# Mixer C's projection steps in another order, and norm weights multiplied in as turned blocks leave PSUM

## The chip, the cores and the metric

The kernel runs on one core of a Trainium2 chip. The metric is the device time of one execution in microseconds (us), the median of several runs. TensorE multiplies and turns, VectorE and ScalarE do the elementwise work, GpSimd takes a small share of it, and SyncE issues all DMA. TensorE has two clock levels, 1.2 and 2.4 GHz; a granted clock of 0.50 in the rows is the lower one, 1.00 the higher.

## The reference

Two layers of a streaming encoder for 1024 prompt frames and 32 sample frames (1056 rows in nine tiles, the last of 32 rows). Each layer normalises x, projects it once for four mixers (A window attention, B differential attention, C latent attention, M cross-attention to 256 memory tokens), attends, projects the concatenated outputs, and ends with a convolutional feed-forward block. What matters here is C, and the queries of M:

```
def _rms(x, g):
    y = xf * lax.rsqrt(jnp.mean(xf * xf, axis=-1, keepdims=True) + EPS)
    return (y * g).astype(x.dtype)

cq = (_rms(cq, w["c_cq_g"]) @ w["c_wuq"]).reshape(B, S, C_HEADS, C_QK)          # rank 256 -> 4 heads x 96
cq = _rms(concatenate([cq[..., :64], _rope(cq[..., 64:], pos)]), w["c_qn_g"])
ckv = _rms(ckv, w["c_ckv_g"])                                                   # rank 128
cpe = _rope(cpe[:, :, None, :], pos)[:, :, 0]                                   # 32 wide, shared by the heads
kv = (ckv @ w["c_wukv"]).reshape(B, nk, C_HEADS, 64 + 64)
ck = _rms(concatenate([kv[..., :64], broadcast(cpe)]), w["c_kn_g"])
mq = _rms(mq.reshape(B, S, M_HEADS, HEAD_DIM), w["m_qn_g"])
```

The norm weight g multiplies after any rotation that stands inside the norm. For the queries and keys of C and the queries of M nothing but the weight comes between the normalised value and the attention, so it can be multiplied in before or after the block is turned.

## The kernel before

A layer runs through stages, each a block with one program per engine: M's projections, M's attention joined with B's projections, B's attention joined with A's projections, A's attention joined with C's projections, C's attention, the output projection (`w_o_block`), the feed-forward (`ffn_block`). Every matmul operand of the dense projections is split in a high and a low part, so each product takes three matmuls (L774 to L776).

`pieces_stage` builds a projection stage from pieces. A piece is one projection (its product, how its columns leave PSUM, its norm, how it is turned and where it goes), with a list of steps (first tile, tiles, rows). C has six pieces: `cq` (5 steps of two tiles, the last of 32 rows; dense, 48 matmuls of 256 columns for a full step), `q_up` (9 steps of one tile, from the turned `c_q_t`, 4 matmuls), `ckv` (5 steps, dense like `cq`, with a rotation of the 32 columns of cpe on VectorE), the prompt's keys (8 steps, 2 matmuls from the turned `ckv_t`), `lat` (4 steps that only turn cached latents) and the sample's keys (5 steps). Queries and keys of C are 4 heads of 96.

`order` is one list of (piece, step) which every engine follows; no planner moves anything. With g a place in this list, the engines' queues are:

- TensorE: product of step g+2, then the turns of step g (L808). A product from a turned tile waits until that tile's blocks have been copied (`placed`). The first two products stand inside the attention that comes before.
- ScalarE: `take(g+1)` copies the product out of PSUM (L855), waits for GpSimd's rotation if there is one, and squares (L866); `place(g-1)` writes the high part of the turned blocks (L894, or L903 for pieces with a plain copy); `root(g+1)` takes the square root (L876).
- VectorE: `results(g)` is a reciprocal (L1011), z by the reciprocal (L1015), by the norm weight (L1025), and for `ckv` the rotation of cpe (L970 to L974); `sum_squares(g+1)` (L992); `low_turned(g-1)`, the low part of the turned blocks (L1049).
- GpSimd: the rotation of the last 32 columns of each q head before the norm (L1079 to L1084).
- SyncE: weights and weights of norms, result writes, in the order of the list. The norm weights are loaded across all partitions, and scaled once (L952) if the piece has a scale.

z, the result and the root have two buffers each, taken in turn by the steps that have a norm. The weights of `ckv` are cast in the last `cq` step (L832, L944). For the keys ScalarE makes three copies: v, the 32 columns of cpe for four heads, and the 64 columns of k.

The order of C before is: the five `cq` steps; then q0, ckv0, q1, q2, ckv1, q3, q4, ckv2, q5, q6, ckv3, q7, q8, ckv4; then eight prompt keys, four `lat`, five sample keys.

## Time and profile before

| | |
|---|---|
| runs | 3252.74, 3257.39, 3262.34 us, median 3257.39 |
| the profiled execution | 3255.39 us, of which the span of the core 3253.6 us |
| TensorE busy | 2920.4 us (90%) |
| VectorE busy | 1807.6 us (56%) |
| ScalarE busy | 1197.6 us (37%) |
| GpSimd busy | 136.5 us (4%) |
| mean granted TensorE clock | 0.936 |
| C's projections after A's attention, first layer | 510 to 617 us |
| the same, second layer | 2111 to 2218 us |

The span is from the first to the last instruction; the execution's own time is 1.8 us more. All starts below are counted from the span's start. Busy times of different engines overlap. A matmul's row gives the modelled duration of one matmul, so rows of successive ones overlap, and the spacing of starts tells how fast they go. In square brackets stands how long the engine was idle before an instruction and what released it.

### The profile page before, as it was taken

How to read it: one execution, taken by the hardware profiler on the slowest of the kernel's cores; microseconds unless marked ns; L12 is line 12 of the kernel's file. 1: busy time of each engine (PE TensorE's matmuls, PEld its weight loads, DVE VectorE, ACT ScalarE, POOL GpSimd, SP SyncE). 2: the span in 40 equal slices, each digit the busy share in tenths (PEclk: the TensorE clock that was granted, in tenths of full speed). 3: DMA queues.
4: the chain of work that ended last, by engine and by line, in shares of the span. 5: the costliest groups of instructions: out<-in, count | busy, mean ns of one | idle time of the engine just before them, and what ended most of it. 6: DMA issues, size and time to landing. Idle time of an engine off the chain costs nothing. (4 is left out here: it accounts for less than half of the span.)

```text
span 3253.6 us, 49067 instructions
## 1 busy us (share of the span) xinstructions
PE 2920.4 (90%) x19080; PEld 2750.4 (85%) x19080; DVE 1807.6 (56%) x2899; ACT 1197.6 (37%) x2503; POOL 136.5 (4%) x228
## 2 busy tenths in 40 slices
PE   5888879789899999999968888788789999999997
PEld 3787768579899999999957868667789999999997
DVE  5466765643555555554665586465436555545554
ACT  5556644652322222222246474456413222212222
POOL 0200012000000000000002000120000000000000
PEclk7996989799999999999979979898899999999999
DMA  4110001022111111111031100110411111111111
GB/s 177 32 57 30 23 29 39 8 86 82 52 46 46 41 50 40 46 45 48 20 124 47 48 22 21 40 29 11 150 28 51 47 45 46 43 50 46 40 46 61
DMA packets 182436, 162.11 MB, mean 50 GB/s; under 512 B 14648, under 2 KB 170040, under 8 KB 181688
## 3 DMA queue, kind: packets, MB, share of 16 engines
q1 hardware_dynamic: 182200, 158.81, 15.5%
q8 instruction: 167, 2.74, 0.4%
q14 instruction: 69, 0.57, 0.1%
HBM read 129.92 MB, written 29.06 MB: 49 GB/s over the span
## 5 line engine op out<-in xcount | busy, mean ns | idle before, releaser
L1752 PE MATMUL ps<-h_hi,w_hi 128*128 128x352 f32 x2496 | 550.5, 329 | 49.6 <-DVE w_lo L1863 23.1
L1752 PE MATMUL ps<-h_hi,w_lo 128*128 128x352 f32 x2496 | 544.6, 325 | 6.9 <-issue 6.9
L1752 PE MATMUL ps<-h_lo,w_hi 128*128 128x352 f32 x2496 | 543.1, 326 | 0.0
L1752 PEld LDWEIGHTS ps<-h_hi,w_hi 128*128 128x128 f32 x2496 | 430.3, 192 | 64.7 <-issue 42.2
L1752 PEld LDWEIGHTS ps<-h_hi,w_lo 128*128 128x128 f32 x2496 | 433.3, 190 | 0.0
L1752 PEld LDWEIGHTS ps<-h_lo,w_hi 128*128 128x128 f32 x2496 | 429.7, 190 | 0.0
L2203 ACT ACTIVATE cv<-up,cols 128x1058 f32<-128x1058 f32 x88 | 112.0, 1273 | 737.9 <-issue 697.8
L774 PE MATMUL ps<-w_hi,h_hi 128*128 128x256 f32 (+1 forms) x1152 | 334.5, 290 | 24.1 <-DVE w_lo L944 18.2
L775 PE MATMUL ps<-w_lo,h_hi 128*128 128x256 f32 (+1 forms) x1152 | 328.8, 285 | 0.0
L776 PE MATMUL ps<-w_hi,h_lo 128*128 128x256 f32 (+1 forms) x1152 | 326.6, 284 | 0.0
L2314 DVE TENSOR_TENSOR x_t<-ps,x_t 128x1056 f32<-128x1056 f32 x176 | 221.0, 1256 | 159.5 <-PE ps L1752 158.8
L2280 DVE TENSOR_TENSOR up<-ps,rinv 128x704 f32<-128x704 f32 x88 | 78.4, 891 | 399.7 <-PE ps L1752 399.7
L1395 ACT ACTIVATE prob<-ps,nm 128x256 f32<-128x256 f32 (+8 forms) x360 | 224.2, 630 | 78.1 <-DVE nm L1309 54.4
L774 PEld LDWEIGHTS ps<-w_hi,h_hi 128*128 128x128 f32 (+1 forms) x1152 | 210.8, 183 | 30.2 <-issue 26.8
L1752 PE MATMUL ps<-act_hi,w_hi 128*128 128x352 f32 x1056 | 229.0, 325 | 5.1 <-issue 5.1
L1752 PE MATMUL ps<-act_lo,w_hi 128*128 128x352 f32 x1056 | 228.1, 324 | 0.0
L1752 PE MATMUL ps<-act_hi,w_lo 128*128 128x352 f32 x1056 | 228.1, 323 | 0.0
L2188 ACT CAST w_hi<-stage 128x1024 fp32r<-128x1024 f32 x132 | 136.0, 1043 | 247.8 <-PE ps L1752 240.8
L776 PEld LDWEIGHTS ps<-w_hi,h_lo 128*128 128x128 f32 (+1 forms) x1152 | 211.8, 184 | 0.9
L775 PEld LDWEIGHTS ps<-w_lo,h_hi 128*128 128x128 f32 (+1 forms) x1152 | 210.8, 183 | 0.8
L1309 DVE TENSOR_REDUCE nm<-ps 32x1 f32<-32x544 f32 (+10 forms) x234 | 184.0, 788 | 33.4 <-PE ps L1216 13.9
L1752 PEld LDWEIGHTS ps<-act_hi,w_hi 128*128 128x128 f32 x1056 | 180.2, 189 | 5.6 <-issue 5.6
(211 smaller groups left out, 4275.7 us busy)
## 6 DMA issues: line engine op xcount, KB each, us to landing
stage<-in_f_win SPq DMA_DIRECT2D x88, 512.0 KB, 3.8
stage<-in_f_wout SPq DMA_DIRECT2D x44, 512.0 KB, 3.7
stage<-in_w_in SPq DMA_DIRECT2D x40, 256.0 KB, 4.4
x_spill<-x_t SPq DMA_DIRECT2D x2, 4224.0 KB, 14.3
x_t<-x_spill SPq DMA_DIRECT2D x2, 4224.0 KB
stage<-in_w_o SPq DMA_DIRECT2D x16, 512.0 KB, 4.5
w_raw<-in_w_in SPq DMA_DIRECT2D x24, 256.0 KB, 3.9
o_in<-o_spill SPq DMA_DIRECT2D x8, 528.0 KB, 7.1
```

The costliest lines, as they stand in the source:

```text
L774: pe.matmul(out, h_hi[:, k, c:c + r], w_hi[:, k, :], start=(k == 0), stop=False)
L775: pe.matmul(out, h_hi[:, k, c:c + r], w_lo[:, k, :], start=False, stop=False)
L776: last = pe.matmul(out, h_lo[:, k, c:c + r], w_hi[:, k, :], start=False, stop=(k == KC - 1))
L1309: dve.tensor_reduce(nm[0:r, j % 4, 0:nh], v, AX.X, ALU.max, negate=True).then_inc(S.nm_done, 1)
L1395: last = act.activation(prob[0:r, j % 4, col:col + kn], src, ACT.Exp, bias=nm[0:r, j % 4, i:i + 1], accum_out=rsum[0:r, j % 4, i:i + 1])
L1752: last = pe.matmul(ps[:, s0 + b, 0:BAND], lh, rh_[:, b * BAND:(b + 1) * BAND], start=(first_k and n == 0), stop=(last_k and n == 2))
L2188: act.copy(w_hi[:, ws, :], stage[:, sg, :]).then_inc(S.hi_done, 1)
L2203: act.activation(cv[:, b, :], up[:, b, 2:UPC], ACT.Identity, scale=cols[:, 1, bass.ds(c, 1)], bias=cols[:, 1, bass.ds(c + 2 * FC, 1)]).the ...
L2280: dve.tensor_tensor(up[:, b, 2:2 + 2 * BAND].rearrange("p (t c) -> p t c", c=BAND), ps[:, s0:s0 + 2, 0:BAND], rinv[:, 0:2 * BAND].rearrang ...
L2314: dve.tensor_tensor(xm, ps[:, s0:s0 + 3, 0:BAND], xm, ALU.add).then_inc(S.x_added, 1)
```

## The change

Four things are changed.

1. A piece may have `late_gain`: C's q and both key pieces, and M's q. Its norm weight is loaded as one column with a value per partition. VectorE's `results` is then one multiplication by the reciprocal, straight into the result; ScalarE's `place` multiplies by the column as it copies, and VectorE's low part is one fused multiply and subtract.
2. C's keys get their 32 shared columns by a GpSimd copy (`shared`), in place of one of ScalarE's three copies. The square waits for it.
3. ScalarE copies k's columns first, then v's.
4. C's order is written out anew: cq0, cq1, cq2, q0, q1, cq3, q2, q3, cq4, q4, q5, ckv0, q6, q7, ckv1, q8, ckv2, k0, k1, lat0, ckv3, k2, k3, lat1, ckv4, k4, k5, lat2, k6, k7, lat3, then the five sample keys.

```diff
         def first_gains(sp):
             for p in normed:
-                sp.dma_start(p.gain_t[:, :], p.gain.partition_broadcast(P)).then_inc(S.small_loaded, 16)
+                if p.late_gain:
+                    for i in range(p.bw // p.hd):
+                        sp.dma_start(p.gain_t[i * p.hd:(i + 1) * p.hd, :], p.gain.rearrange("(h o) -> h o", o=1)
+                                     ).then_inc(S.small_loaded, 16)
+                else:
+                    sp.dma_start(p.gain_t[:, :], p.gain.partition_broadcast(P)).then_inc(S.small_loaded, 16)
...
-                    if p.rope_first:
+                    if p.rope_first or p.shared is not None:
                         act.wait_ge(S.pre_rotated, rot_i[g] + 1)
...
-                            act.copy(hi, src).then_inc(S.tr_copied, 1)
+                            if p.late_gain:
+                                if s == 0:
+                                    act.wait_ge(S.small_loaded, n_small)
+                                    if n_scaled[id(p)]:
+                                        act.wait_ge(S.gain_scaled, n_scaled[id(p)])
+                                act.mul(hi, src, p.gain_t[0:p.bw, 0:1]).then_inc(S.tr_copied, 1)
+                            else:
+                                act.copy(hi, src).then_inc(S.tr_copied, 1)
...
+                    if p.late_gain:
+                        dve.tensor_tensor(res[0:r, n % 2, 0:nt * n_el].rearrange("p (t h d) -> p t h d", t=nt, d=hd),
+                                          zv[:, :, 0:n_el].rearrange("p t (h d) -> p t h d", d=hd),
+                                          ri[0:r, 0:gh].rearrange("p (t h) -> p t h", t=nt).unsqueeze(3).broadcast_to([r, nt, H, hd]),
+                                          ALU.mult).then_inc(S.res_done, 1)
+                        return
...
-                    dve.tensor_tensor(lo, src, hi.bitcast(F32), ALU.subtract).then_inc(S.tr_low, 1)
+                    if p.late_gain:
+                        dve.scalar_tensor_tensor(lo, src, p.gain_t[0:p.bw, 0:1], hi.bitcast(F32), ALU.mult, ALU.subtract
+                                                 ).then_inc(S.tr_low, 1)
+                    else:
+                        dve.tensor_tensor(lo, src, hi.bitcast(F32), ALU.subtract).then_inc(S.tr_low, 1)
...
-                steps = [g for g in range(NG) if G[g][0].rope_first]
+                steps = [g for g in range(NG) if G[g][0].rope_first or G[g][0].shared is not None]
...
+                    if p.shared is not None:
+                        src, from_load, producer = p.shared(s)
+                        pool.wait_ge(S.res_done, n_i[g] - 1)
+                        if from_load:
+                            pool.wait_ge(S.data_loaded0, 16 * len(late_loads))
+                        else:
+                            q, qs = producer
+                            pool.wait_ge(S.res_done, n_i[at[id(q), qs]] + 1)
+                        zp = zs[0:r, n_i[g] % 2, 0:p.n_el].rearrange("p (h c) -> p h c", c=p.hd)
+                        pool.tensor_copy(zp[:, :, 64:96], src.unsqueeze(1).broadcast_to([r, 4, 32])).then_inc(S.pre_rotated, 1)
+                        continue
...
-                return [(v_big[0:r, v_tile(t0), :].rearrange("p (h c) -> p h c", c=64), b4[:, :, 64:128]),
-                        (z4[:, :, 64:96], cpe_of(t0, r).unsqueeze(1).broadcast_to([r, 4, 32])),
-                        (z4[:, :, 0:64], b4[:, :, 0:64])]
+                return [(z4[:, :, 0:64], b4[:, :, 0:64]),
+                        (v_big[0:r, v_tile(t0), :].rearrange("p (h c) -> p h c", c=64), b4[:, :, 64:128])]
...
-        order = [(cq, s) for s in range(5)]
-        for s in range(5):
-            order += [(q_up, 2 * s), (ckv, s)] + ([(q_up, 2 * s + 1)] if s < 4 else [])
-        order += [(p, s) for p in pieces[3:] for s in range(len(p.steps))]
+        k_p, k_c = pieces[3], pieces[5]
+        order = [(cq, 0), (cq, 1), (cq, 2), (q_up, 0), (q_up, 1), (cq, 3), (q_up, 2), (q_up, 3), (cq, 4), (q_up, 4), (q_up, 5),
+                 (ckv, 0), (q_up, 6), (q_up, 7), (ckv, 1), (q_up, 8), (ckv, 2), (k_p, 0), (k_p, 1), (lat, 0), (ckv, 3),
+                 (k_p, 2), (k_p, 3), (lat, 1), (ckv, 4), (k_p, 4), (k_p, 5), (lat, 2), (k_p, 6), (k_p, 7), (lat, 3)]
+        order += [(k_c, s) for s in range(5)]
```

## Rows read from the trace of the kernel before

**Rows 1.** Stretches of C's projections: length, busy (count) per engine, PEclk, DMA share, GB/s.

```profile
538.00:549.00 11.00, 10.09 (x70) 8.42 (x70) 6.91 (x19) 4.75 (x14) 4.65 (x11) 1.00 0.07 17
578.00:598.50 20.50, 14.10 (x47) 6.33 (x47) 19.09 (x50) 16.25 (x50) 0.00 (x0) 0.83 0.01 2
```

**Rows 2.** Timeline of the stage's end: start, duration, engine, line, instruction, count.

```profile
614.29 0.30 ACT L876 ACTIVATE rt<-ss,eps_c 32x4 f32<-32x4 f32 x1 [0.29 <-DVE ss L992]
...
617.02 0.29 DVE L1049 TENSOR_TENSOR kc_s<-ps,kc_s 96x128 fp32r<-96x128 f32 x1 [0.31 <-ACT kc_s L894]
```

**Rows 3.** TensorE's timeline over one period of ckv and two q steps.

```profile
537.83 0.44 PE L808 MATMUL ps<-ident,res 128*128 128x128 f32 x2 [0.86 <-DVE cpe_all L974]
...
543.84 0.60 PE L808 MATMUL ps<-ident,res 128*96 128x128 f32 x4
...
548.49 0.44 PE L808 MATMUL ps<-ident,res 128*128 128x128 f32 x2 [0.91 <-DVE cpe_all L974]
```

**Rows 4.** ScalarE's timeline over the same period, the roots.

```profile
539.46 0.30 ACT L876 ACTIVATE rt<-ss,eps_c 128x4 f32<-128x4 f32 x1
...
543.81 0.30 ACT L876 ACTIVATE rt<-ss,eps_c 128x4 f32<-128x4 f32 x1 [0.30 <-DVE ss L992]
...
545.96 0.30 ACT L876 ACTIVATE rt<-ss,eps_c 128x2 f32<-128x2 f32 x1 [0.57 <-DVE ss L992]
```

**Rows 5.** Timeline of one key step on ScalarE and VectorE.

```profile
582.80 0.30 ACT L876 ACTIVATE rt<-ss,eps_c 128x4 f32<-128x4 f32 x1 [0.63 <-DVE ss L992]
...
583.44 0.56 DVE L1015 TENSOR_TENSOR u<-zs,ri 128x384 f32<-128x384 f32 x1
...
584.03 0.56 DVE L1025 TENSOR_TENSOR res<-u,gain 128x384 f32<-128x384 f32 x1
...
584.97 0.68 DVE L1049 TENSOR_TENSOR k_st<-ps,k_st 96x512 fp32r<-96x512 f32 x1
...
585.77 0.56 DVE L1015 TENSOR_TENSOR u<-zs,ri 128x384 f32<-128x384 f32 x1
```

**Rows 6.** Lines of the output projection: duration in ns min/median/max, first and last start.

```profile
L1831 ACT ACTIVATE h_hi<-ps,subln_c x12: 287/682/691, 745.2 to 2348.9; 128x512 fp32r<-128x512 f32 x8, 128x32 fp32r<-128x32 f32 x4
L1833 ACT CAST h_hi<-ps x12: 186/587/595, 735.7 to 2339.3; 128x512 fp32r<-128x512 f32 x8, 128x32 fp32r<-128x32 f32 x4
L1875 DVE SCALAR_TENSOR_TENSOR h_lo<-ps,subln_c,h_hi x12: 250/742/751, 746.4 to 2349.3; 128x512 fp32r<-128x512 f32 x8, 128x32 fp32r<-128x32 f32 x4
```

**Rows 7.** Timeline of the first sample key step on ScalarE and VectorE.

```profile
603.59 0.52 ACT L866 ACTIVATE sq<-zs 128x384 f32<-128x384 f32 x1
...
604.14 0.55 DVE L992 TENSOR_REDUCE ss<-sq 128x4 f32<-128x384 f32 x1 [3.10 <-ACT sq L866]
604.73 0.30 ACT L876 ACTIVATE rt<-ss,eps_c 128x4 f32<-128x4 f32 x1 [0.47 <-DVE ss L992]
...
605.79 0.52 ACT L866 ACTIVATE sq<-zs 128x384 f32<-128x384 f32 x1
```

**Rows 8.** ScalarE's timeline at the end of the cq steps.

```profile
517.24 0.63 ACT L903 COPY c_q_t<-ps 128x256 f32<-128x256 f32 x2
518.09 0.30 ACT L876 ACTIVATE rt<-ss,eps_c 128x2 f32<-128x2 f32 x1 [0.22 <-DVE ss L992]
...
525.69 2.17 ACT L832 CAST w_hi<-stage 128x512 fp32r<-128x512 f32 x4
```

**Rows 9.** VectorE's timeline at the end of M's projections.

```profile
110.25 0.41 DVE L1025 TENSOR_TENSOR res<-u,gain 32x256 f32<-32x256 f32 x1
```

**Rows 10.** Stretches around a change of the granted clock, columns as in rows 1.

```profile
574.40:577.80 3.40, 0.81 (x2) 0.00 (x0) 1.73 (x5) 2.07 (x7) 0.44 (x1) 1.00 0.00 0
577.80:584.50 6.70, 6.58 (x15) 2.86 (x15) 5.70 (x20) 4.97 (x18) 0.00 (x0) 0.50 0.02 3
```

**Rows 11.** C's attention in the first and the second layer, columns as in rows 1.

```profile
618.40:711.00 92.60, 92.05 (x660) 85.09 (x660) 43.54 (x140) 51.27 (x129) 0.00 (x0) 0.89 0.04 13
2219.00:2311.00 92.00, 87.29 (x660) 80.90 (x660) 43.60 (x141) 51.26 (x129) 0.00 (x0) 0.93 0.05 14
```

More of the change, by code:

```diff
@@ L161, in build_program @@
         loads_done = sem("loads_done")
+        gain_scaled = sem("gain_scaled")
         fin_done = sem("fin_done")
@@ L495, in piece @@
                  rope_first=False, rope_extra=False, gain=None, scale=None, cached=None, raw=None, stack=None, to=None,
-                 res_out=None, v_out=None, placed=None)
+                 res_out=None, v_out=None, placed=None, late_gain=False, shared=None)
         p.update(args)
@@ L514, in __init__ @@
             self.gain_t, self.scale = None, p["scale"]
+            self.late_gain, self.shared = p["late_gain"], p["shared"]
         @property
@@ L581, in pieces_stage @@
         for p in normed:
-            p.gain_t = (gains or w).take("gain", [P, p.hd])
+            p.gain_t = (gains or w).take("gain", [P, 1 if p.late_gain else p.hd])
         G = order or [(p, s) for p in pieces for s in range(len(p.steps))]
@@ L606, in pieces_stage @@
         a_i = count(lambda p: p.after)
-        rot_i = count(lambda p: p.rope_first)
+        rot_i = count(lambda p: p.rope_first or p.shared is not None)
         normed_steps = [g for g in range(NG) if G[g][0].normed]
@@ L623, in pieces_stage @@
                     split_after[last_of[id(holders[i - 1])]] = p
-        n_small = 16 * len(normed)
+        n_small = 16 * sum(p.bw // p.hd if p.late_gain else 1 for p in normed)
         n_loads = 16 * len(loads)
+        n_scaled, scaled = {}, 0
+        for p in normed:
+            scaled += 1 if p.scale is not None else 0
+            n_scaled[id(p)] = scaled
         res_sem = (S.res_out0, S.res_out1)
@@ L1078, in gpsimd @@
                         pool.wait_ge(S.pre_rotated, i)
+                    turned_steps += 1
                     pool.tensor_tensor(a[:, :, 0:16], x1, cos, ALU.mult)
@@ L1581, in group_m @@
             piece(PAIRS, w_col=COL["mq"], copies=zs_copy, zsw=256, H=4, hd=HD, gain=I["m_qn_g"][layer], scale=HD ** -0.5,
-                  stack="after", to=lambda t: (q2_hi, q2_lo, t * P)),
+                  late_gain=True, stack="after", to=lambda t: (q2_hi, q2_lo, t * P)),
             piece([(0, 1, P), (1, 1, P)], H=4, hd=HD, cached=lambda s: kc[:, s, :],
@@ L1706, in pieces_c, with keys @@
         lat = piece([(t, 1, P) for t in range(4)], raw=lambda s: lat_in[:, s, :], stack="raw", to=lambda t: (ckv_s, None, t * P))
-        def keys(steps, latents, cpe_of, v_tile, placed, to):
+        def keys(steps, latents, shared, v_tile, placed, to):
             def product(pe, t, r, out):
@@ L1714, in copies @@
                 z4 = zs.rearrange("p t (h c) -> p (t h) c", c=96)
-                return [(v_big[0:r, v_tile(t0), :].rearrange("p (h c) -> p h c", c=64), b4[:, :, 64:128]),
-                        (z4[:, :, 64:96], cpe_of(t0, r).unsqueeze(1).broadcast_to([r, 4, 32])),
-                        (z4[:, :, 0:64], b4[:, :, 0:64])]
+                return [(z4[:, :, 0:64], b4[:, :, 0:64]),
+                        (v_big[0:r, v_tile(t0), :].rearrange("p (h c) -> p h c", c=64), b4[:, :, 64:128])]
             return piece(steps, product=product, placed=placed, zw=512, zsw=384, copies=copies, H=4, hd=96,
-                         gain=I["c_kn_g"][layer], stack="after96", to=to)
+                         gain=I["c_kn_g"][layer], stack="after96", to=to, late_gain=True, shared=shared)
         pieces = [
             cq, q_up, ckv,
-            keys(SINGLES[:-1], lambda t, r: ckv_t[:, t * P:t * P + r], lambda t, r: cpe_all[0:r, t, :], lambda t: t,
+            keys(SINGLES[:-1], lambda t, r: ckv_t[:, t * P:t * P + r], lambda s: (cpe_all[:, s, :], False, (ckv, s // 2)), lambda t: t,
                  lambda s: (ckv, s // 2), lambda t: (k_st[:, 0::2, :], k_st[:, 1::2, :], t * P)),
@@ L1728, in pieces_c @@
                  lambda t, r: ckv_s[:, t * P:t * P + r] if t < 4 else ckv_t[:, SEQ:T],
-                 lambda t, r: cpe_s[0:r, t, :] if t < 4 else cpe_all[0:r, PT_TILES, :], lambda t: PT_TILES + t,
+                 lambda s: (cpe_s[:, s, :], True, None) if s < 4 else (cpe_all[0:DEC, PT_TILES, :], False, (ckv, 4)),
+                 lambda t: PT_TILES + t,
                  lambda s: (lat, s) if s < 4 else (ckv, 4), lambda t: (k_s[:, 0::2, :], k_s[:, 1::2, :], t * P)),
         ]
-        order = [(cq, s) for s in range(5)]
-        for s in range(5):
-            order += [(q_up, 2 * s), (ckv, s)] + ([(q_up, 2 * s + 1)] if s < 4 else [])
-        order += [(p, s) for p in pieces[3:] for s in range(len(p.steps))]
+        k_p, k_c = pieces[3], pieces[5]
[3 more added lines that the diff above has]
+        order += [(k_c, s) for s in range(5)]
         return pieces_stage(layer, pieces, R_W2, order=order, joint=FOUR_HEADS,
```

9 lines of the change are left out of this document (7 added, 2 removed).

## Prediction

> **What bounds the kernel now.** I read the table of busy times first: TensorE works 90% of the span, VectorE 56%, ScalarE 37%. That is an average over stages, so I cut the stage of mixer C into stretches [rows 1]. Up to 571 us TensorE is busy 10.09 of 11 us; later it is not: from 578 to 598.5 it is busy 14.10 of 20.5, part of that at the low clock of 1.2 GHz (granted 0.83 in the mean), and VectorE is the full one, 19.09 of 20.5. So the stage has a dense part, set by TensorE or near it, and a light part of some 45 us after the last ckv product, set by the chain of the norm: ScalarE copies z out of PSUM, squares it, VectorE sums, ScalarE takes the root, VectorE scales, TensorE turns, ScalarE and VectorE write high and low part. The stage's last write ends at 617.31 [rows 2]. The second layer has the same stage, 108 us long too.
>
> Then the timeline of one period with two q steps and one ckv step [rows 3]: turns of ckv stand at 537.83 and 548.49, 10.66 us apart, and TensorE is idle 0.86 and 0.91 us before them, for VectorE's last rotary add. The dense product takes 538.02 to 543.84, 5.82 us. The reader is to see that even the dense part hangs on the chain, by a little. ScalarE's roots give the chain's pitch [rows 4]: 539.46 to 543.81 is 4.35 us for a second q step, 543.81 to 545.96 is 2.15 for ckv, and what is left of the 10.66 is 4.16 for the other q step. (A q step is long because ScalarE waits in it until GpSimd has rotated.)
>
> A key step lasts 2.33 us [rows 5], from 583.44 to 585.77 on VectorE, which has no idle time between.
>
> **Late weights (the gain).** 22 steps of a layer in C (9 q, 13 keys) and 5 in M lose VectorE's multiplication by the gain: 0.59 us from 583.44 to 584.03 is what it adds before the result is there [rows 5], 0.35 for 32 rows of M. Instead the place on ScalarE takes a per-partition factor, and the low part becomes a fused multiply and subtract. The trace has both forms in the output projection [rows 6]: 682 against 587 ns on ScalarE, 742 ns on VectorE against the 0.68 of the plain subtract in [rows 5]. So +0.10 and +0.06 us a step. ScalarE's extra lies beside the sum and root of the same step (the square starts 1.14 before the root [rows 7], square and place take 0.43 + 0.67 of it), so it costs nothing there; if the cover fails, 22 x 0.1 = 2.2 us a layer.
>
> **GpSimd copies the shared key part.** One of three copies leaves ScalarE's key step, 0.20 us of the 1.06 from a root to the next square [rows 7]. The new GpSimd copy of 128 x 128 is not in the trace: nothing if hidden, 0.5 us if exposed (ScalarE's own copy of it is the nearest: its 0.20 is the spacing, so 0.5 is a bound with a wait's latency in it). It may start when the result of two steps before is there, a whole step early, so I take nothing.
>
> **New pitch of a key step.** In [rows 7], where the sum did not queue behind VectorE's other work: square 603.59, root 604.73 (1.14), next square 605.79 (1.06 with three copies, 0.86 with two). So 2.00 us, ScalarE and VectorE in turn; VectorE's own work is 2.33 - 0.59 + 0.06 = 1.80, so it no longer sets it. A ckv step after q steps falls from 2.15 to 1.65, since the q result it queues behind comes 0.59 earlier and the longer place takes back 0.1.
>
> **The new order.** TensorE's queue is: product of step g+2, then turn of g. I follow the roots from 518.09, which both kernels share [rows 8].
> - q0 now stands right after cq2. Its product needs cq0's blocks in c_q_t, written at 517.24 + 0.63 = 517.87 [rows 8]. Product 1.4, so the copy is at 519.45, and its root at 519.45 + 3.95 = 523.4. New stall, TensorE idle 1.6.
> - q1 4.35, cq3 2.2, q2 4.16, q3 4.35: 538.4. cq4 carries the cast of the ckv weights, 2.17 on ScalarE [rows 8] and as long again on VectorE behind it: 4.1, so 542.5. q4, q5 8.5: 551.0. ckv0 1.65, q6, q7 8.5, ckv1 1.65, q8 4.4: 567.3.
> - ckv1's product could start 2.72 after ckv0's root, 555.4, and ends at 561.2; then come a turn, q8's product and q7's turn, 2.2 (two turns and two products take 3.74 in [rows 3], 4.65 less the idle 0.91). ckv2's product runs 563.4 to 569.25, so here TensorE is the later one by 2.0.
> - Now the critical place. From the end E of a dense ckv product: copy, square, sum and root start 0.2, 0.46, 0.45 and 0.44 after one another (from the spacings of these rows and the half width of ckv's), so root at E + 1.55; the turn comes 2.53 after the root (545.96 to 548.49, [rows 3, 4]). VectorE is free for the sum of the first key step only then (E + 3.92), its root follows 0.59 later [rows 7], at E + 4.5, and its turn after 1.25 (582.80 to 583.44, 0.56 of work, 0.05 to the turn [rows 5]), and after 0.45 of turning, E + 6.2, TensorE may start the product of ckv3: the lat step beside it has no product, so ckv3 stands in TensorE's queue behind the turn of that key step. The period is 5.82 + 6.2 = 12.0, not the some 9 us that the products and turns would fill. So ckv3 runs 575.5 to 581.3, ckv4 (32 rows, half as long) 587.6 to 590.6.
> - Root of the fifth key step: 590.6 + 3.8 = 594.4, by the same steps with the 32-row results of ckv4, an estimate. Eight key steps remain at 2.0, and the product after a lat step is late twice by about 0.8, as it waits for the turn of the key step three before: 594.4 + 16 + 1.6 = 612.0. From the last root, 614.29, to the end took 3.0 in the old kernel [rows 2], now 0.59 less: 614.4.
>
> The old order had one more cost that goes: the four lat turns stood in one row, with VectorE idle 3.10 us before the sum of 604.14 [rows 7].
>
> Sum in C: 617.3 to 614.4, -2.9 us a layer. Much of what the interleaving hides (ckv3 and ckv4 beside key steps) comes back as waits of 5.7 and 2.8 us of those steps for the dense products.
>
> In M the projection's tail ends on the chain: the gain at 110.25, 0.41 us before the last results, is gone [rows 9], and the mul costs 0.1: -0.35. One more small load in M's queue, about 0.5 us of SyncE, lies ahead of w_mem, whose first use is later than its landing by the copies of mem_t; if that cover is gone, +0.5. C's gain loads are as many as before (five), and 4-byte rows; no step needs them for 50 us. The late loads of C now start at ckv0, 542 us, and the first key product is at 570: hidden.
>
> Work of both layers: 2 x (-2.9 - 0.35) = -6.5 us.
>
> **The clock.** TensorE was busy 0.81 of 3.40 us, then the granted clock fell to 0.50 and stayed there for 6.7 us [rows 10]. Today that falls on a light part that VectorE sets, and costs little. In the new order each lull after a dense ckv product (little to do in its last 3.7 us but two turns) is followed by a dense product, which at 1.2 GHz takes twice as long: 6.7 us of it cost 3.4. The light part from 578 to 598.5, idle a third of its time, was granted 0.83: such a lull is sometimes followed by the fall and sometimes not [rows 1]. There are two such lulls before ckv3 and ckv4 and a smaller one before ckv0. I take one fall a layer that costs 2 us after what other waits absorb: +4. Bounds: 0, and three a layer, 2 x (3.4 + 3.4 + 3) = +19.6.
>
> The Trainium skill, "TensorE: Matmul & The Clock Gate", section "HAM oscillation — how this bites in real kernels", says that bursts of matmuls parted by waits can run at the low clock each time anew, and it advises to keep dense work together. That speaks against this order. By it every lull would be paid, which is the upper bound, +19.6; by the rows, of which the periods with gaps of 0.9 us ran at 1.00 throughout [rows 1], only some.
>
> The profiled execution took 3255.39 us, 1.8 above its span and 2.0 below the median 3257.39. Its sum: 3255.4 - 6.5 + 4 = 3252.9; on the median's footing 3254.9. I say 3254.
>
> **Rivals.**
> 1. *The worked chain, one fall a layer (the forecast)*: 3254, own range 3248 to 3259. Chance 0.50.
> 2. *No fall under a dense product*: 3257.4 - 6.5 = 3251. For it: the q periods kept 1.00 with their gaps. Chance 0.20.
> 3. *The lull is filled*: the first key step's sum gets ahead of ckv's rotation, or the product of ckv3 is issued before that turn. Then each period is about 9 instead of 12, twice a layer, and the key steps wait less: -12 more, 3239. Against it: both queues are in written order. Also here: C's attention starts at half clock for longer in the first layer than in the second, TensorE 92.05 against 87.29 us busy for the same 660 matmuls [rows 11]; if the first gets the short one, -4.8 more. Together 0.18 for 3236 to 3247.
> 4. *Slower: the clock falls in every lull before a dense product.* Place: ckv0, ckv3 and ckv4 of both layers; price 19.6 in all, 3257.4 - 6.5 + 19.6 = 3270.5. It decides once the falls cost over 6.5 + 9.8 = 16.3 us, so nearly all have to come. For it: the fall at 577.8 came after just such a lull. Against it: products of q and keys still stand in most of the lull. Chance 0.12. The rule of the Trainium skill quoted above gives this outcome.
>
> **Numbers.** A measurement of this kernel can tell about 0.3%, 9.8 us, from no change: 3247.6 and 3267.2. Faster: nearly all of rival 3 and a bit of 2, 0.21. Slower: 0.09 of rival 4 and an unforeseen wait, 0.10. Same: 0.69. Range: from within rival 3 to short of rival 4's end, 3240 to 3266.
>
> **What would show it.** The stage from 510 us to the end of key writes in C should last about 105 us instead of 107.3; the gain's multiplication should be gone from q and key steps; key roots 2.0 apart at the end; TensorE idle about 1.6 us before the first q product; 6.2 us from the end of ckv2's product to the start of ckv3's; lat turns without a wait of their own; whether the clock is 0.50 within ckv3. I am wrong if the lull before ckv3 is much shorter, if q periods are no longer 10.2 to 10.7 us, or if the place with a factor lands on the chain.

## The result and the profile after

The kernel after takes 3293.42 us (3273.57 to 3310.11, 13 runs) against 3257.68 of the kernel before (3249.49 to 3285.07, 13 runs): a ratio of 1.0096, 95% interval 1.0071 to 1.0121. It is slower, and above the forecast's range. The profiled execution took 3294.7 us, 39.3 more than that of before; the mean granted clock fell from 0.936 to 0.926.

TensorE's busy time rose by 32 us (2920.4 before), for the same 19080 matmuls:

```profile
PE 2952.1 (90%) x19080; PEld 2785.4 (85%) x19080; DVE 1784.9 (54%) x2845; ACT 1196.7 (36%) x2477; POOL 141.1 (4%) x254
```

C's attention in both layers, the stretches of [rows 11] (length, busy per engine, granted clock, DMA share, GB/s):

```profile
621.86:736.05 114.19, 114.18 (x660) 105.43 (x660) 43.23 (x139) 51.02 (x129) 0.00 (x0) 0.70 0.03 10
2243.05:2349.28 106.23, 106.22 (x660) 97.98 (x660) 43.23 (x139) 51.10 (x129) 0.00 (x0) 0.76 0.03 11
```

From its first to its last matmul it lasts 114.19 and 106.23 us where it lasted 92.06 and 87.29: +41.1 us, more than the whole loss. The change does not touch this stage. Cut at the changes of the clock (the return stands at 689.73), first layer, kernel after:

```profile
618.04:621.86 3.82, 0.58 (x5) 0.42 (x5) 2.29 (x5) 1.18 (x4) 0.00 (x0) 0.50 0.00 0
621.86:689.90 68.04, 68.04 (x280) 63.74 (x281) 24.74 (x90) 27.00 (x74) 0.00 (x0) 0.50 0.03 8
689.90:736.05 46.15, 46.14 (x382) 41.69 (x381) 18.48 (x49) 24.02 (x56) 0.00 (x0) 1.00 0.04 12
```

and of the kernel before:

```profile
615.37:618.43 3.06, 0.53 (x4) 0.42 (x5) 1.59 (x4) 0.30 (x2) 0.00 (x0) 0.50 0.00 0
618.43:639.20 20.77, 20.77 (x86) 19.59 (x86) 10.75 (x47) 10.18 (x34) 0.00 (x0) 0.50 0.04 13
639.20:710.49 71.29, 71.29 (x577) 65.47 (x575) 32.52 (x93) 41.05 (x95) 0.00 (x0) 1.00 0.04 12
```

In both the clock falls in the light tail, 3 to 4 us before the attention. Then TensorE is busy without a gap, yet stays at 0.50 for 20.8 us in one kernel and 68.0 in the other. The Trainium skill ("TensorE: Matmul & The Clock Gate", Part 1) has the granted clock follow how busy TensorE has lately been. A row of 68.04 us busy in 68.04 at 0.50 does not agree, if busy is read as the profile shows it.

The projections themselves, kernel after. TensorE waits before q0's product, and between ckv2's product (it ends at 572.86, where a turn follows) and the first matmul of ckv3's (578.86):

```profile
520.66 1.53 PE L1740 MATMUL ps<-w_uq,c_q_t 128*128 128x384 f32 x4 [1.52 <-ACT c_q_t L921]
...
576.78 0.44 PE L819 MATMUL ps<-ident,res 128*128 128x128 f32 x2 [1.32 <-DVE cpe_all L994]
578.47 0.64 PE L819 MATMUL ps<-ident,res 128*96 128x128 f32 x4 [1.25 <-DVE res L1036]
578.86 0.36 PE L785 MATMUL ps<-w_hi,h_hi 128*128 128x256 f32 x1
```

Key steps and the stage's end, on ScalarE, VectorE and GpSimd, answering to [rows 2] and [rows 5]: the gain's multiplication is gone, the low part takes 0.74 us, the GpSimd copy 0.29.

```profile
577.22 0.30 ACT L887 ACTIVATE rt<-ss,eps_c 128x4 f32<-128x4 f32 x1 [1.16 <-DVE ss L1012]
577.86 0.56 DVE L1036 TENSOR_TENSOR res<-zs,ri 128x384 f32<-128x384 f32 x1
579.22 0.30 ACT L887 ACTIVATE rt<-ss,eps_c 128x4 f32<-128x4 f32 x1 [0.30 <-DVE ss L1012]
580.34 0.74 DVE L1077 SCALAR_TENSOR_TENSOR k_st<-ps,gain,k_st 96x512 fp32r<-96x512 f32 x1
580.48 0.29 POOL L1111 COPY zs<-cpe_all 128x128 f32<-128x128 f32 x1 [3.41 <-DVE res L1036]
...
617.96 0.30 ACT L887 ACTIVATE rt<-ss,eps_c 32x4 f32<-32x4 f32 x1
620.37 0.34 DVE L1077 SCALAR_TENSOR_TENSOR kc_s<-ps,gain,kc_s 96x128 fp32r<-96x128 f32 x1 [0.35 <-ACT kc_s L910]
```

The clock at 0.50 inside the projections of the first layer, where ckv0's product takes 7.1 us in place of 5.8 and ckv4's 4.2 in place of some 3:

```profile
543.10:549.90 6.80, 5.43 (x20) 3.92 (x19) 4.76 (x12) 3.80 (x9) 2.20 (x6) 0.51 0.35 87
590.90:594.30 3.40, 3.40 (x18) 2.84 (x17) 1.83 (x4) 1.14 (x3) 0.29 (x1) 0.52 0.00 0
```

### The profile page after: what moved, and what is told of

It is laid out like the page before. It is cut to its first block and busy times, and to the rows that moved or that the text cites. A ratio compares the mean times of both kernels' runs of the same rounds, so it can differ in the third digit from the quotient of the medians.

```text
span 3292.9 us, 49051 instructions
## 1 busy us (share of the span) xinstructions
PE 2952.1 (90%) x19080; PEld 2785.4 (85%) x19080; DVE 1784.9 (54%) x2845; ACT 1196.7 (36%) x2477; POOL 141.1 (4%) x254
## 5 line engine op out<-in xcount | busy, mean ns | idle before, releaser
L1456 ACT COPY pt<-ps 128x512 f32<-128x512 f32 (+5 forms) x306 | 127.7, 457 | 181.3 <-PE ps L1279 181.3
```

The source lines that it names most:

```text
L1456: act.copy(pt[0:kn, p % 2, grp[0]:grp[0] + len(grp), 0:r], ps[0:kn, 4 + g % 2, 0:len(grp) * P].rearrange("p (m c) -> p m c", c=P)[:, :, 0: ...
```

## The experiments

Eighteen more kernels were measured. Four measures are read from each profile, beside the time. "Proj" is the work of C's projections, from the root of cq2 to the last root (518.09 to 614.29 before: 96.2 us). "Att" is C's attention from first to last matmul, first/second layer. "Start" is where that first matmul stands against the last fall of the clock before it or the first one inside the attention: +3.1 is 3.1 us behind it, -2.0 means that the clock fell 2.0 us into the attention. "Low" is the time at 0.50 inside the attention. The moments of fall and return are read to a few hundredths of a us, from stretches that end or begin there. Times taken at different hours differ by some us; each ratio is against runs of before taken beside it.

| kernel | us (range, runs) | ratio to before, 95% | Proj | Att | Start | Low |
|---|---|---|---|---|---|---|
| before, profiled run | 3255.39 | | 96.2/96.2 | 92.1/87.3 | +3.1/+3.0 | 21/11 |
| after, profiled run | 3294.70 | | 97.2/97.2 | 114.2/106.2 | +3.8/+3.7 | 68/51 |
| e1 old order, late weights | 3234.39 (3226.83-3249.02, 10) | 0.9924 [0.9892, 0.9955] | 89.4/89.4 | 87.4/87.3 | +2.8/+2.9 | 11/11 |
| e2 new order alone | 3263.18 (3259.19-3291.45, 10) | 1.0025 [0.9987, 1.0063] | 102.6/102.7 | 90.8/87.4 | +2.4/+2.8 | 18/11 |
| e3 after, filled | 3237.55 (3231.74-3277.61, 10) | 0.9964 [0.9928, 0.9999] | 99.9/99.9 | 83.2/83.2 | no fall | 0/0 |
| e4 before, filled | 3254.25 (3229.68-3269.26, 10) | 0.9969 [0.9929, 1.0009] | 96.2/96.4 | 86.1/115.0 | -2.9/-3.1 | 7/68 |
| f1 before, 0.6 us wait | 3281.36 (3260.45-3305.42, 8) | 1.0079 [1.0050, 1.0109] | 96.2/96.2 | 114.3/91.8 | +3.7/+3.5 | 68/20 |
| f2 after, 1.1 us wait | 3265.97 (3254.21-3275.72, 10) | 1.0025 [1.0008, 1.0042] | 100.0/97.3 | 96.2/96.0 | +4.5/+5.0 | 30/29 |
| f3 after, 2.2 us wait | 3262.90 (3254.84-3267.49, 10) | 1.0020 [1.0010, 1.0030] | 97.3/97.4 | 87.4/92.1 | +6.2/+6.5 | 11/21 |
| f4 e1, filled | 3223.10 (3220.42-3231.80, 4) | 0.9910 [0.9892, 0.9929] | 88.4/88.4 | 91.9/87.3 | +3.3/+3.0 | 21/11 |
| g1 e1, lat turns between keys | 3236.64 (3232.53-3268.77, 10) | 0.9931 [0.9894, 0.9967] | 89.0/89.1 | 90.8/116.6 | +2.3/+2.2 | 18/73 |
| g2 e1 without GpSimd's copy | 3249.21 (3243.55-3261.09, 10) | 0.9973 [0.9939, 1.0006] | 92.2/92.3 | 90.9/95.8 | +2.3/+1.9 | 18/29 |
| g3 f4, B filled too | 3222.97 (3219.71-3229.01, 4) | 0.9886 [0.9810, 0.9961] | 90.6/88.4 | 83.2/92.0 | none/+3.3 | 0/21 |
| g4 new order up to ckv2 | 3267.33 (3241.64-3288.72, 10) | 1.0015 [0.9972, 1.0057] | 92.9/94.4 | 114.2/104.4 | +3.7/+4.2 | 68/47 |
| h1 e1, 0.6 us wait | 3246.95 (3240.20-3275.20, 11) | 0.9973 [0.9947, 0.9998] | 89.4/89.4 | 106.2/106.3 | +3.7/+3.6 | 51/51 |
| h2 after, filled at the end only | 3266.88 (3255.06-3297.20, 10) | 1.0038 [1.0007, 1.0070] | 97.4/100.0 | 95.5/103.6 | -1.6/-1.8 | 27/44 |
| h3 e1, filled more | 3214.42 (3207.69-3223.20, 4) | 0.9865 [0.9819, 0.9912] | 88.8/88.8 | 83.2/83.2 | no fall | 0/0 |
| h4 g1, filled more | 3219.05 (3216.22-3221.31, 4) | 0.9875 [0.9834, 0.9917] | 89.0/89.1 | 83.2/83.2 | no fall | 0/0 |
| i1 before, filled more | 3274.58 (3259.07-3285.74, 12) | 1.0060 [1.0037, 1.0083] | 95.3/96.8 | 108.4/105.2 | -2.0/-2.1 | 55/48 |
| i2 after, filled more | 3238.39 (3235.70-3260.35, 11) | 0.9960 [0.9940, 0.9981] | 96.3/96.2 | 89.3/86.1 | -3.0/-2.9 | 14/7 |

### Undo the order, or make it alone (e1, e2)

e1 is the kernel after with the old list:

```diff
-        k_p, k_c = pieces[3], pieces[5]
-        order = [(cq, 0), (cq, 1), (cq, 2), (q_up, 0), ...
+        order = [(cq, s) for s in range(5)]
+        for s in range(5):
+            order += [(q_up, 2 * s), (ckv, s)] + ([(q_up, 2 * s + 1)] if s < 4 else [])
+        order += [(p, s) for p in pieces[3:] for s in range(len(p.steps))]
```

> The kernel after with C's order put back to the old one; the late norm weights, the smaller projection pieces of ScalarE and GpSimd's copy of the shared columns stay. Where the two profiles differ by 39 us, some 42 us lie in C's attention, whose instructions are the same in both: it stays at the granted clock 0.50 for 71.7 and 54.6 us from the fall before it, against 23.9 and 13.7 us. Theory A, the new order brings this (the steps before the attention come at another rhythm): here it is gone, and what is left is the shorter steps, 3250 to 3258 us. Theory B, the short key steps at the stage's end bring it (turns 2.0 us apart in place of 2.33): it stays, 3280 to 3300. Theory C, neither edit but the moment at which the attention starts: the time scatters by 20 us and more from run to run, anywhere from 3250 to 3300, and the span goes with the mean granted clock.

e2 is the kernel before with the new list.

> The kernel before with the new order alone: norm weights and ScalarE's three copies of a key step as before, key steps 2.33 us. Theory A (the order): C's attention stays at 0.50 for over 50 us, 3285 to 3305 us. Theory B (the short key steps): attention as before, and the stage itself about as long as in the kernel before or some 2 us longer, 3255 to 3265. Theory C (the moment of the start): scatter of 20 us and more from run to run.

e1 came out 20 us below the kernel before, beyond what theory A gave. e2's median, 3263.18 us, lies in theory B's range, but not for B's reason: its projections are 6.4 us a layer longer where B had at most 2, and two of its ten runs, 3285 and 3291, lie where A had put all of them. Proj gives the work: late weights and the smaller key step take 6.8 us a layer off in the old order (96.2 to 89.4) and 5.4 in the new one (102.6 to 97.2); the new order costs 6.4 with early weights and 7.8 with late ones. Nothing of this is 41 us. A and B both fell: the new order alone has a short stay at 0.50 (18 and 11 us, against A), and so have the short key steps in the old order (11 and 11, against B).

The roots around the turns of the cached latents in e1 (ScalarE), and its attention:

```profile
589.06 0.30 ACT L887 ACTIVATE rt<-ss,eps_c 128x4 f32<-128x4 f32 x1
591.06 0.30 ACT L887 ACTIVATE rt<-ss,eps_c 128x4 f32<-128x4 f32 x1
598.10 0.30 ACT L887 ACTIVATE rt<-ss,eps_c 128x4 f32<-128x4 f32 x1 [0.47 <-DVE ss L1012]
```

```profile
609.98:697.34 87.36, 87.35 (x660) 80.93 (x660) 43.28 (x139) 51.20 (x129) 0.00 (x0) 0.94 0.04 13
2200.62:2287.96 87.34, 87.34 (x660) 80.92 (x660) 43.28 (x139) 51.19 (x129) 0.00 (x0) 0.94 0.04 13
```

A key step is 2.00 us here, as worked out.

### Fill the tail (e3, e4)

```diff
+                    if len(late_loads) == 3 and g >= NG - 9:
+                        warm(pe, 2)          # pe.matmul(ps[:, 0, 0:512], h_hi[:, 0, 0:P], h_hi[:, 0, 0:512]), unread
                     turn(g)
+                if len(late_loads) == 3:
+                    warm(pe, 6)
```

> The kernel after with extra matmuls at the end of C's projections, whose results nobody reads: two of 128 x 512 before each of the last nine turns, six behind the last one, where TensorE otherwise waits. Theory D, the attention is slow because the clock has already fallen in the light tail ahead of it: with the tail filled the clock is 1.00 when the attention starts, and stays there; both attentions lose all their time at 0.50, (71.7 + 54.6) x 0.47 = 59 us, some 3235 to 3240 us. Against it: the attention itself is what cannot hold the clock; then it falls anyway soon after the start, and the time is 3285 to 3310.

> The kernel before with the same extra matmuls. Theory D: (23.9 + 13.7) x 0.47 = 18 us less, 3238 to 3242 us, which would put it level with the same filling in the kernel after, less the 6 us of work that the change takes out. Otherwise 3255 to 3300 with the clock at 0.50 in the attention as often as before.

e3 took 56 us less than the kernel after (3293.42, at another hour), with no work removed. Its attention never falls:

```profile
621.62:704.79 83.17, 82.93 (x660) 76.17 (x660) 43.28 (x139) 50.95 (x129) 0.00 (x0) 1.00 0.04 14
```

So 83.2 us is this attention at full clock, and each us at 0.50 adds 0.39 to 0.46 ((87.3 - 83.2) / 10.6, (114.2 - 83.2) / 68.0). In e4 the filling carried the clock over the start, but it fell 2.9 and 3.1 us later and stayed down for 68.3 us in the second layer. Its ten times lie from 3230 to 3269, their median 3254.25 above the 3238 to 3242 expected. Filling acts on the cause, but does not hold the clock in every run.

### Move nothing but the start (f1, f2, f3, h1)

```diff
                 low_turned(NG - 1)
+                if len(late_loads) == 3:
+                    for _ in range(1):       # f1, h1: 1, f2: 2, f3: 4
+                        link(dve.tensor_tensor(u[:, 0:384], sq[:, 0:384], sq[:, 0:384], ALU.mult))
```

The extra multiplications stand behind everything else that VectorE does for C's projections, so they put off the attention and nothing ahead of it.

> The kernel before with one extra VectorE multiplication of 128 x 384 (some 0.56 us), read by nobody, behind the last low part of C's projections: C's attention starts that much later, nothing else moves. In the profiles so far the attention starts 3.13 and 3.0 us behind the moment at which the granted clock fell in the kernel before, and goes back to 1.00 after 20.8 and 10.7 us; in the kernel with the old order and late weights 2.98 and 3.02 us behind it, back after 10.7 and 10.7; with the new order alone 2.25 and 2.56, back after 18.2 and 11.1; in the kernel after 3.66 and 3.45, back after 68 and 51 us. Theory E, what decides is where the start lies against the moment of the fall: here it lies 3.6 us behind it, the attention stays at 0.50 for over 40 us a layer, and the time goes up by 20 to 45 us, to 3275 to 3300. Rival F, it is what the tail of the stage does (shorter steps, other distances of turns): nothing but the added time, 3254.1 + 1.1 = 3255.

> The kernel after with two such multiplications (1.1 us) behind the last low part. Theory E: the start moves from 3.55 to 4.7 us behind the fall; the attention should find the clock back sooner, and the time falls by 20 to 40 us to 3252 to 3275, though 1.1 us a layer are added. Rival F: 3293 + 2 = 3295.

> The same with four (2.2 us). Theory E: again a shorter stay at 0.50, 3253 to 3275; two waits of different length both helping would say that only a narrow place of the start is bad. Rival F: 3293 + 4 = 3297.

> Old order, late weights and GpSimd's copy (3234 us; its attention starts 3.0 us behind the fall and is back at 1.00 after 10.7 us in both layers), with one VectorE multiplication of some 0.56 us behind the last low part. Theory E (the place of the start decides, and 3.4 to 3.7 us behind the fall is a bad one in the kernels before and after): 51 to 68 us at 0.50, 20 to 27 us more a layer, 3260 to 3290 us. Rival: this stage's tail is robust, and the gain of 20 us is its own: 3235 to 3240.

f1, the kernel before with 0.54 us of idle work on VectorE, has in its first layer the kernel after's attention, all but instruction for instruction (280 and 281 matmuls in the low stretch); in the second it stays low for 20 us:

```profile
617.73 0.54 DVE L1062 TENSOR_TENSOR u<-sq 128x384 f32<-128x384 f32 x1
```

```profile
615.89:619.63 3.74, 0.53 (x5) 0.42 (x5) 2.04 (x5) 0.30 (x2) 0.00 (x0) 0.50 0.00 0
619.63:687.80 68.17, 68.17 (x281) 63.87 (x281) 24.77 (x90) 27.17 (x75) 0.00 (x0) 0.50 0.03 8
```

It lost 26 us in the median for 1.1 us of added work. And the kernel after gets faster by waiting: 27 us with 1.1 us a layer, 31 with 2.2, against the 3293.42 of an earlier hour (f3's attention, both layers):

```profile
624.15:711.54 87.39, 87.39 (x660) 80.97 (x660) 43.29 (x139) 51.25 (x129) 0.00 (x0) 0.94 0.04 13
2225.28:2317.36 92.08, 92.07 (x660) 85.09 (x660) 43.29 (x139) 51.24 (x129) 0.00 (x0) 0.89 0.04 12
```

Rival F, that the content of the tail decides, is out: in these kernels it is the same. Theory E holds in direction. The distances in its text (3.66, 2.98 and so on) came from coarser stretches; read at the fall itself they are those of the table. Second layers of f1 and h1, and the first of the kernel after:

```profile
2240.43:2240.63 0.20, 0.00 (x0) 0.00 (x0) 0.17 (x2) 0.00 (x0) 0.00 (x0) 1.00 0.00 0
2240.63:2244.15 3.52, 0.52 (x4) 0.42 (x5) 1.83 (x4) 0.30 (x2) 0.00 (x0) 0.50 0.00 0
2218.64:2218.84 0.20, 0.00 (x0) 0.00 (x0) 0.17 (x2) 0.12 (x1) 0.00 (x0) 1.00 0.00 0
2218.84:2222.47 3.63, 0.53 (x4) 0.42 (x5) 1.93 (x4) 0.40 (x2) 0.00 (x0) 0.50 0.00 0
617.84:618.04 0.20, 0.20 (x3) 0.00 (x0) 0.17 (x2) 0.16 (x2) 0.00 (x0) 1.00 0.17 41
```

Of the forty attentions in the twenty profiles, 25 start while the clock is down from a fall ahead of them. In order of the distance, with kernels described further down:

| start behind the fall, us | low, us | attentions |
|---|---|---|
| 1.91 | 29 | g2 second |
| 2.20 | 73 | g1 second |
| 2.34 to 2.40 | 18 | g1, g2 and e2 first |
| 2.75 to 3.00 | 11 | e2 second, e1 both, f4 second, before second |
| 3.06 to 3.52 | 20 to 21 | before first, g3 second, f4 first, f1 second |
| 3.63 to 3.68 | 51 | h1 both, after second |
| 3.70 to 3.82 | 68 | g4 first, f1 first, after first |
| 4.19 | 47 | g4 second |
| 4.52, 4.97 | 30, 29 | f2 |
| 6.17, 6.45 | 11, 21 | f3 |

Different kernels share a row. So in these profiles the distance tells how long the clock stays down, and between 3.52 and 3.63 us the stay jumps from 20 to 51. This orders 25 starts; it does not say why.

The times of theory E are less sure: h1 lost 12.6 us against e1, not 26 to 56; its profiled run, 3275.20 with 51 us low in both layers, is the slowest of eleven, and eight of the others show a mean clock of 0.939 or 0.940, close to e1's. Where their attentions started against the fall is not known, as only the profiled run has a trace.

### What each part of the work is worth (g1, g2, g4)

g2 puts ScalarE's three copies back into e1, g4 changes the new list behind ckv2, and g1 takes the old list to ckv4 and then spreads the cached latents:

```diff
 # g2
-                return [(z4[:, :, 0:64], b4[:, :, 0:64]),
-                        (v_big[0:r, v_tile(t0), :]..., b4[:, :, 64:128])]
+                return [(v_big[0:r, v_tile(t0), :]..., b4[:, :, 64:128]),
+                        (z4[:, :, 64:96], cpe_of(t0, r).unsqueeze(1).broadcast_to([r, 4, 32])),
+                        (z4[:, :, 0:64], b4[:, :, 0:64])]
 # g4
-                 (ckv, 0), (q_up, 6), (q_up, 7), (ckv, 1), (q_up, 8), (ckv, 2), (k_p, 0), (k_p, 1), (lat, 0), (ckv, 3), ...
+                 (ckv, 0), (q_up, 6), (q_up, 7), (ckv, 1), (q_up, 8), (ckv, 2), (ckv, 3), (ckv, 4)]
+        order += [(p, s) for p in pieces[3:] for s in range(len(p.steps))]
 # g1
+        for s in range(4):
+            order += [(k_p, 2 * s), (k_p, 2 * s + 1), (lat, s)]
```

> Old order, late norm weights, but ScalarE makes its three copies of a key step in the old order and GpSimd none. My working gave a key step 1.06 + 1.14 = 2.20 us where ScalarE and VectorE take turns, against 2.00 with two copies and 2.33 before. Then 13 x 0.2 = 2.6 us a layer of the gain are the GpSimd copy's, and the stage lasts 2.6 us longer than with both. If GpSimd's copy is worth nothing because VectorE or the wait for it sets the step, the roots stand 2.00 apart here too.

> The kernel after with the new order of cq, q and ckv up to ckv2, then ckv3, ckv4, and keys and cached latents as in the old order. From the root of cq2 to the last root of C's projections the kernel after takes 97.2 us, the old order with late weights 89.4. Theory G, the cost of 7.8 us lies between ckv2 and the last key (waits before ckv3 and ckv4, a dense product behind a key's turn): here 90 to 92. Theory H, it lies in the early q steps (1.5 us stall before q0, q steps while the next cq weights are cast): here 95 to 97.

> The kernel after with the old order up to ckv4, then the turns of cached latents one behind each two prompt keys as in the new order, then the sample's keys. In the old order with late weights the roots on both sides of the four turns stand at 591.06 and 598.10, 7.04 us apart where 2.00 is a key step; in the new order one such turn costs 0.8 us (607.15 to 609.98). So the stage should last 5.0 - 4 x 0.8 = 1.8 us a layer less than with the old order, 105.6 where the old order has 107.4 or so. The total depends besides on where the attention's start falls against the clock: if about 3.0 us behind the fall as in the old order, 3231; if the fall stays and the start moves to 1 or 4.5 us behind it, anything from 3230 to 3265.

g2's key roots stand 2.20 apart, as expected:

```profile
578.61 0.30 ACT L887 ACTIVATE rt<-ss,eps_c 128x4 f32<-128x4 f32 x1 [0.79 <-DVE ss L1012]
580.82 0.30 ACT L887 ACTIVATE rt<-ss,eps_c 128x4 f32<-128x4 f32 x1 [0.55 <-DVE ss L1012]
583.02 0.30 ACT L887 ACTIVATE rt<-ss,eps_c 128x4 f32<-128x4 f32 x1
```

So of the 6.8 us a layer, 4.0 are the late weights' (96.2 to 92.2) and 2.8 those of GpSimd's copy with the smaller ScalarE step. (g2 also puts back the old sequence of ScalarE's copies, v first, so the two are not told apart.) g4 stands between G and H: 3.5 us lie in the early part (first layer; the second, with a fall of the clock in it, 5.0), the other 4.3 between ckv2 and the last key, the clock's price on ckv4 among them. g1 gained 0.4 us, not 1.8: the key steps behind the four lat turns take 3.9, 2.6, 2.9 and 2.8 us and one more 2.5 in place of 2.0 each, 4.7 in all, nearly the 5.0 that four turns in a row cost.

### Filling again, and a version faster than both (f4, g3, h2, h3, h4, i1, i2)

f4 is e1 with e3's filling; g3 adds six matmuls behind B's projections; h2 is the kernel after with `warm(pe, 14)` at the end and none between turns; h3 (on e1), h4 (on g1), i1 (on before) and i2 (on after) fill more:

```diff
-                    if len(late_loads) == 3 and g >= NG - 9:
-                        warm(pe, 2)
+                    if len(late_loads) == 3 and g >= NG - 13:    # h2: warm(pe, 0)
+                        warm(pe, 3)
                     turn(g)
-                if len(late_loads) == 3:
-                    warm(pe, 6)
+                if len(late_loads) == 3:                         # g3: or over_results is not None, warm(pe, 6)
+                    warm(pe, 8)                                  # h2: 14
```

> Old order, late norm weights and GpSimd's copy (3234 us by itself), with the extra matmuls at the stage's end. The first of these had C's attention at 0.50 for 10.7 us a layer. If the filling holds the clock as it did in the kernel after (3293 to 3238), 2 x 10.7 x 0.47 = 10 us less: 3224 to 3228. If it fails in some runs as in the kernel before (3230 to 3236 or 3261 to 3269), two groups of times, 3225 and 3255, and a median anywhere between.

> Old order, late weights, GpSimd's copy and the extra matmuls in C (3223 us), with six more of 128 x 512 behind the last turn of B's projections. B's attention starts at 0.50 in all profiles, 44.4 and 37.5 us of it in the kernel before, on a stretch where VectorE is as full as TensorE. If the extra matmuls keep the clock up, some 5 to 20 us less, 3205 to 3218; if B's attention cannot hold it, no change.

> The kernel after with fourteen matmuls of 128 x 512 behind the last turn, none between the turns. If the tail between the turns is where the clock falls, it falls all the same 3 to 4 us before the attention, the fourteen run at 0.50 (0.43 us each, some 6 us, about 3 us more than the wait that is there today), and the attention starts later and at another place: 3250 to 3300, the profile tells. If it is the gap behind the last turn alone that brings the fall, no fall: 3293 - 2 x 27 = 3240.

> Old order with late weights; three matmuls of 128 x 512 before each of the last thirteen turns and eight behind the last one (two, nine and six in the kernel of 3223 us, whose profile still showed falls 3.3 and 3.0 us before the attention). If that holds the clock: C's attention 83.2 us in both layers, where the profile of 3223 us had 91.9 and 87.3: 13 us less, 3210. The filling may cost up to 0.2 us a key step where TensorE had too little room, 5 us in all: 3215. If the clock falls anyway, 3223 to 3250.

> The same filling with the turns of the cached latents between the prompt keys (3237 us without filling; from the root of cq2 to the last root 89.0 us against 89.4). Held clock: 3210 to 3214, within 1 us of the one before. Without it, anything up to 3260.

> The kernel before with three extra matmuls of 128 x 512 before each of the last thirteen turns of C's projections and eight behind the last. If C's attention is held at 1.00 in both layers: 83.2 us each in place of 92.1 and 87.3, 13 us less, 3242 us, or some 14 more than the old order with late weights and the same filling, since its stage is 6.8 us a layer longer: 3214 + 14 = 3228. The two ways disagree by 14 us; which is right says how much of 3214 comes from elsewhere. If the fall comes just behind the attention's start, as in the first filling of this kernel: up to 3265.

> The kernel after with the same filling. Held clock: 3237 as with the lighter filling, or up to 5 us more where the filling takes room that dense products want. Against the kernel before with the same filling: from the root of cq2 to the last root it took 99.9 us with the lighter filling against 96.2, so it should be 2 x 3.7 = 7 us slower; without any filling the two stood at 97.2 and 96.2, 2 us. That is the change without the clock: no gain, a loss of 2 to 7 us.

f4's attention started behind falls as e1's did, so its 11 us below e1 are not explained by C's attention; the two were also measured at different hours. Filling B changed nothing that can be told (3223.1 and 3223.0). h2 shows the tail between the turns to be where the clock goes: with the end filled alone it fell all the same, 8.7 and 8.4 us before the attention, came back, and fell again inside it. h3 is the fastest of all, 1.35% below the kernel before (0.9865, 0.9819 to 0.9912, four runs), with the clock at 1.00 in both attentions:

```profile
608.13:691.33 83.20, 82.95 (x660) 76.20 (x660) 43.28 (x139) 50.94 (x129) 0.00 (x0) 1.00 0.04 14
2191.72:2274.89 83.17, 82.93 (x660) 76.18 (x660) 43.27 (x139) 50.93 (x129) 0.00 (x0) 1.00 0.04 14
```

h4 has both attentions at 83.2 us too, but took 3219.05 us, above the 3210 to 3214 expected; its ratio of 0.9875 (0.9834 to 0.9917) can't be told from h3's.

The same filling in the kernel before is no remedy: i1 was meant to show the work with the clock taken out, and failed at that. In its first layer, the filled gap, the attention's first 2 us, and what follows:

```profile
618.50:623.10 4.60, 3.50 (x8) 2.42 (x9) 0.39 (x2) 0.30 (x2) 0.00 (x0) 0.66 0.00 0
623.10:625.10 2.00, 1.75 (x13) 1.62 (x14) 1.28 (x7) 1.99 (x6) 0.00 (x0) 0.99 0.04 8
625.10:679.70 54.60, 54.60 (x224) 50.89 (x224) 20.66 (x75) 21.25 (x62) 0.00 (x0) 0.50 0.03 10
```

and i2's attentions:

```profile
617.24:706.55 89.31, 89.06 (x660) 82.02 (x660) 43.28 (x139) 50.91 (x129) 0.00 (x0) 0.92 0.04 13
2211.40:2297.54 86.14, 85.89 (x660) 79.19 (x660) 43.28 (x139) 50.91 (x129) 0.00 (x0) 0.96 0.04 14
```

With one filling in both, the kernel after (i2) is 36 us faster than the kernel before (i1); without it, 36 us slower. The sign of the comparison is the clock's. By its work the change is about nothing: taking from each profiled execution what its attentions exceed 2 x 83.2 us leaves 3242 for before and 3241 for after. The same sum gives 3235 for i1 and 3228 for i2, and 3226 for e4 and 3232 for e3, so it is sure to some 7 us only, either way.

## Why the prediction was wrong

**The step that failed** is "The clock". It priced a fall only where one of C's dense products runs under it (+4 us, 19.6 at most), and its fourth rival summed those falls alone. What fell and stayed low was the stage behind, C's attention: +41.1 us in the profiled run. The row that could have warned was on the table: 92.05 and 87.29 us for the same 660 matmuls [rows 11]. I used it as a possible gain of 4.8 us in rival 3 and set no loss against it. Had I asked how long that stay could get, the bound would have been the whole attention at 1.2 GHz; from the rows of before alone, 92.05 us at a mean of 0.89, nothing excluded it. This one term is nearly the whole miss: in the terms of the profiled runs the forecast was 3252.9, and 3294.70 is 41.8 above it.

**The outcome** had the sign of rival 4 but not its mechanism. The rule of the Trainium skill quoted there ("TensorE: Matmul & The Clock Gate", section "HAM oscillation — how this bites in real kernels"), lulls before dense work, came true only in part: the clock did fall over ckv0 and ckv4 (row 543.10 and row 590.90), and ckv3 ran at full clock (it lies between). In the projections that cost 1.3 and some 1.2 us a layer, near the 2 that I took.

**The stage** went nearly as worked out. In the kernel before's time (the cq2 root stands at 520.74 in the kernel after, 2.65 later): root of q0 523.1, worked out 523.4; q3 538.3 against 538.4; cq4 542.3 against 542.5; ckv2 571.8 against 570.8 (569.25 + 1.55); the stall before q0 1.52 us against 1.6; from ckv2's product to ckv3's 6.0 against 6.2. One size was off and hidden by others: a ckv step among q steps took 2.55 and 2.47 us (roots 553.01 to 555.56, 563.79 to 566.26), not 1.65, while two q steps took 8.1 to 8.2, not 8.5. Then it drifts: last root 615.3 against 612.0. About 2.5 of these 3.3 us are the two slowed products; 0.8 stays unexplained. The end of key writes came at 618.1 (620.71 less 2.65), not 614.4: the stage got 0.8 us longer rather than 2.9 shorter, and 2 of this difference of 3.7 were in the clock's term already.

**Late weights and the GpSimd copy**: right, key step 2.00 us (g2: 2.20 without the copy). That they were worth 6.8 us a layer and the order took it all back the forecast had only as a net; e1 shows that the better half alone was there to have.

**Rival 3, the lull filled**, did not come: the first key's sum queued behind ckv's rotation. Its second half, a short low stay in the first layer's attention too, turned into the opposite.

**M**: the traces settle it, though no run changed M alone. From the last root of M's projections to the first matmul of its attention it took 4.73 us before and 4.46 after (4.71 and 4.46 in the second layer), so the change is worth 0.26 us a layer against 0.35 worked out:

```profile
108.98 0.30 ACT L876 ACTIVATE rt<-ss,eps_c 32x4 f32<-32x4 f32 x1
113.71 0.58 PE L1207 MATMUL ps<-mk_hi,q_hi 64*128 64x256 f32 x2 [2.10 <-PEq L223]
108.61 0.29 ACT L887 ACTIVATE rt<-ss,eps_c 32x4 f32<-32x4 f32 x1
113.07 0.58 PE L1252 MATMUL ps<-mk_hi,q_hi 64*128 64x256 f32 x2 [2.12 <-PEq L224]
```

**What stays open**: why the clock comes back when it does. The table of distances gives the same stay for the same distance in different kernels, but not in one direction: 73 us at 2.20, 11 at 2.75 to 3.00, 68 at 3.70 to 3.82, 11 again at 6.17. Several of its rows have one or two starts only, and it says nothing of the falls inside an attention (1.6 to 2.1 us behind the start gave 27 to 55 us low, 2.9 to 3.1 gave 7, 7, 14 and 68). That most of the 13 runs of the kernel after share the long stay is read from their mean clocks (0.921 to 0.931), not from traces.

## What to carry to other kernels

Where a light tail leads into a stage that keeps TensorE busy at a low clock, price that whole stage at either level before moving anything ahead of it. Before crediting or blaming an edit, add a wait of half a microsecond to the old kernel: if that alone moves the time by more than the edit should, read the work from stretches at equal clock. Time the parts of a change apart: one half of this one was a gain of 0.8% by itself.

## What the runs showed of the hardware that was not expected

- TensorE busy 68.04 of 68.04 us stayed at a granted clock of 0.50; an unbroken busy row is no sign that the clock will return.
- The attention took 114.2 us with 68.0 at 0.50 and 83.2 with none, so the low stretch did the work of 37.0 us (83.2 less the other 46.2) and took 1.84 times as long; one of 10.6 us did the work of 6.5, 1.6 times. So the price of one us at 0.50 was not the same in the two.
- 0.54 us of VectorE work ahead of the stage cost 26 us of the kernel; 2.2 us ahead of it in the other kernel saved 31.
- The same 660 matmuls spent 20 us at 0.50 when they started 3.52 us behind a fall of the clock and 51 when they started 3.63 behind it (f1 and h1, second layers).
- In the eleven profiles without extra matmuls the clock fell at nearly the same distance before the attention in both layers (3.1 and 3.0, 3.8 and 3.7, 2.8 and 2.9, 2.3 and 2.2; 0.5 us apart at most). That where it falls is a property of the kernel is suggested by this, not shown, as each kernel has one trace.
